# Expert stage of a hybrid encoder layer on one Trainium2 core: the loop over slots written out, and each expert number read once

## What is computed

```python
def _hier_moe(x, w_rg, b_rg, w_re, b_re, w1, w3, w2):
    ...
    y = jnp.zeros(t.shape, jnp.float32)
    for e in range(N_EXPERTS):
        he = jax.nn.silu(t @ w1[e]) * (t @ w3[e])
        y = y + gates[:, e:e + 1] * (he @ w2[e]).astype(jnp.float32)
    return y.reshape(B, S, D).astype(x.dtype)
```

## Time and profile before

| what | value |
| --- | --- |
| median of 3 runs | 1200.32 us (1195.77 to 1204.63) |
| the profiled execution | 1196.12 us, of which the span from first to last instruction is 1194.2 us |
| PE busy over the span | 1065.5 us (89%) |
| DVE, ACT, POOL busy | 697.2, 525.4, 344.9 us |
| mean granted clock of PE | 0.962 |
| DMA, mean over the span | 203 GB/s |
| DMA on SP's queue (q1), on POOL's (q0) | 117.42 MB, 122.17 MB |

### The profile page before, as it was taken

One profiled execution on the slowest core, in us unless ns is written; L12 is line 12 of the kernel. 1 busy time (PEld: TensorE's weight loads), 2 busy tenths in 40 slices (PEclk: granted clock), 3 DMA queues, 4 the chain that ended last, 5 costly groups with the idle time before them and its releaser, 6 DMA issues.

```text
span 1194.2 us, 18236 instructions
## 1 busy us (share of the span) xinstructions
PE 1065.5 (89%) x5777; PEld 860.0 (72%) x5777; DVE 697.2 (58%) x1326; ACT 525.4 (44%) x1025; POOL 344.9 (29%) x368
## 2 busy tenths in 40 slices
PE   5999999998987899999999999975999999999940
PEld 4889889984555777777778777863777777777830
DVE  4330610118666667576575655448777777787867
ACT  4432421213532333323333333313787878788823
POOL 3100510000541111111110100201656565666655
PEclk9999999999989999899999999996999999999985
DMA  7340141122579586465555444834988687877667
GB/s 273 118 164 1 45 127 64 45 78 68 195 272 364 199 322 244 174 229 207 205 198 198 156 170 151 295 143 160 302 313 325 243 282 248 284 253 255 246 240 278
DMA packets 105764, 242.83 MB, mean 203 GB/s; under 512 B 15248, under 2 KB 63840, under 8 KB 95456
## 3 DMA queue, kind: packets, MB, share of 16 engines
q1 hardware_dynamic: 81312, 117.42, 28.8%
q0 software_dynamic: 23328, 122.17, 28.7%
q10 hardware_dynamic: 1056, 2.36, 0.6%
HBM read 243.31 MB, written 48.94 MB: 245 GB/s over the span
## 4 chain that ended last, share of the span: by engine, by line
PE 58%; DMA 12%; DVE 9%; issue 8%; ACT 5%; SPq 5%; POOL 2%; POOLq 0%; DVEq 0%; ACTq 0%
DMA below<-in_w 8%; PE ps L1076 5%; PE ps L2189 4%; PE ps L2191 4%; PE ps L2190 4%; PE ps L929 4%; PE ps L947 3%; SPq L1426 3%; PE ps L1117 3%; PE ps L1025 3%; PE ps L1118 3%; PE ps L2184 3%; PE ps L2183 3%; PE ps L2185 3%; PE ps L1121 3%
## 5 line engine op out<-in xcount | busy, mean ns | idle before, releaser
L1842 DVE TENSOR_TENSOR low<-below,high 128x1024 fp32r<-128x1024 f32 x128 | 156.6, 1260 | 35.3 <-ACT high L1539 31.8
L1638 PE MATMUL ps<-high 128*128 128x512 f32 x384 | 156.1, 407 | 10.8 <-DVE low L1852 7.2
L1514 POOL TENSOR_TENSOR low<-below,high 128x1024 fp32r<-128x1024 f32 x62 | 129.0, 2081 | 94.0 <-ACT high L1559 93.1
L1639 PE MATMUL ps<-low,high 128*128 128x512 f32 x384 | 150.7, 392 | 0.0
L1640 PE MATMUL ps<-high,low 128*128 128x512 f32 x384 | 150.6, 392 | 0.0
L1539 ACT ACTIVATE high<-below 128x1024 fp32r<-128x1024 f32 x128 | 130.3, 1070 | 38.6 <-DMA below<-in_w 37.9
L653 ACT ACTIVATE arena<-ps 128x512 f32<-128x512 f32 (+8 forms) x100 | 50.1, 511 | 172.0 <-PE ps L929 171.6
L929 PE MATMUL ps<-arena 128*128 128x128 f32 (+4 forms) x613 | 94.3, 277 | 7.5 <-ACT arena L653 2.2
L797 POOL DMA_DIRECT2D high<-wo_dram x34 | 18.7, 549 | 281.6 <-PE ps L1121 270.8
L1638 PEld LDWEIGHTS ps<-high 128*128 128x128 f32 x384 | 72.5, 189 | 28.1 <-issue 12.8
L947 PE MATMUL ps<-arena 128*128 128x64 f32 (+2 forms) x624 | 83.4, 269 | 6.9 <-DVE arena L702 2.9
(11 more groups left out here) (251 smaller groups left out, 2215.8 us busy)
## 6 DMA issues: line engine op xcount, KB each, us to landing
below<-in_w SPq DMA_DIRECT2D x256, 256.0 KB
high<-wo_dram POOLq DMA_DIRECT2D x36, 1024.0 KB, 5.9
low<-wo_dram POOLq DMA_DIRECT2D x36, 1024.0 KB, 8.6
below<-in_w POOLq DMA_DIRECT2D x64, 512.0 KB
y_dram<-arena SPq DMA_DIRECT2D x32, 512.0 KB
arena<-in_x_prompt SPq DMA_DIRECT2D x15, 512.0 KB
below<-in_w_in SPq DMA_DIRECT2D x14, 512.0 KB, 7.7
out<-arena SPq DMA_DIRECT2D x9, 512.0 KB, 2.7
```

Of the source, the lines that this page charges most:

```text
L1514: pool.tensor_tensor(w2_lo[s % UN][:, c], w2_in[:, c], w2_hi[s % UN][:, c].bitcast(F32), ALU.subtract).then_inc(s_w2lo, 1)
L1638: pe.matmul(out, x_hi, w_hi, start=start, stop=False)
L1639: pe.matmul(out, x_hi, w_lo, start=False, stop=False)
L1842: dve.tensor_tensor(chunk(w13_lo[j], c), chunk(w13_in, c), chunk(w13_hi[j], c).bitcast(F32), ALU.subtract).then_inc(s_w13lo, 1)
```

## The change

`expert_turns` is replaced by `expert_slots`, which writes all 32 slots out for ACT, PE and DVE, with every slot number a constant. SP's body becomes a plain loop over 32 slots that is written out in the same way. `expert` takes the number of the slot before as an argument (a register that was loaded a slot earlier) and loads only one number. On SP the number of slot s+1 is read after the loads of slot s are issued and ahead of the wait for the output rows of s-3; the second wait for `s_etab`, which had been there in every slot, goes. On POOL it is read after the gather and ahead of the two subtractions. What each engine computes, and in which order, is otherwise as it was.

```diff
-    def expert_turns(eng, body):
-
-        turns = SLOT_TILES // UN - 1
-        assert SLOT_TILES % UN == 0
-        for it in range(2):
-            for j in range(UN):
-                body(it, j, it == 0, False)
-        with eng.Fori(2, turns - 1) as it:
-            for j in range(UN):
-                body(it, j, False, False)
-        for it in (turns - 1, turns):
-            for j in range(UN):
-                body(it, j, False, it == turns and j == UN - 1)
+    def expert_slots(body):
+
+        for s in range(SLOT_TILES):
+            body(s // UN, s % UN, s < UN, s == SLOT_TILES - 1)
...
-    def expert(eng, s):
-
-        e = eng.value_load(expert_of[0:1, bass.ds(s, 1)], min_val=0, max_val=NE - 1)
-        if is_zero(s):
-            return e, None
-        return e, e != eng.value_load(expert_of[0:1, bass.ds(s - 1, 1)], min_val=0, max_val=NE - 1)
+    def expert(eng, s, e_before):
+
+        e = eng.value_load(expert_of[0:1, s:s + 1], min_val=0, max_val=NE - 1)
+        return e, None if e_before is None else e != e_before
 
     def moe_loads(sp):
...
         sp.wait_ge(s_etab, 1)
-
-        def body(it, j, first, last):
-            s = it * UN + j
-            e, new = expert(sp, s)
+        e, new = expert(sp, 0, None)
+        for s in range(SLOT_TILES):
+            j = s % UN
             rows13 = [w[0, bass.ds(e, 1)].rearrange("e (c p) f -> p (e c) f", p=P) for w in (w1, w3)]
             for c in range(WC):
 
-                if not is_zero(s):
-                    split = sp.to_reg(WC * (s - 1) + c + 1)
-                    if c == 0:
-
-                        sp.wait_ge(s_etab, 1)
-
-                    sp.wait_ge(s_w13lo, split)
+                if s:
+                    sp.wait_ge(s_w13lo, WC * (s - 1) + c + 1)
                 for k in range(2):
                     sp.dma_start(w13_in[:, 2 * c:2 * c + 2, k * FF:(k + 1) * FF], rows13[k][:, 2 * c:2 * c + 2, :],
                                  cond=new).then_inc(s_w13in[c], 16)
-            if not isinstance(s, int) or s >= 3:
+            if s + 1 < SLOT_TILES:
+                e, new = expert(sp, s + 1, e)
+            if s >= 3:
                 store_y(s - 3)
...
-        def load_second(s):
-            e, new = expert(pool, s)
+        def load_second(s, e, new):
...
             if s + 1 < SLOT_TILES:
+                e, new = expert(pool, s + 1, e)
                 for c in range(2):
                     pool.wait_ge(s_w2hi, 2 * s + c + 1)
                     pool.tensor_tensor(w2_lo[s % UN][:, c], w2_in[:, c], w2_hi[s % UN][:, c].bitcast(F32),
                                        ALU.subtract).then_inc(s_w2lo, 1)
-                load_second(s + 1)
+                load_second(s + 1, e, new)
```

More of the change, by code:

```diff
@@ L1400, in chunk @@
         return w[:, 2 * c:2 * c + 2, :]
-    def expert(eng, s):
-        e = eng.value_load(expert_of[0:1, bass.ds(s, 1)], min_val=0, max_val=NE - 1)
-        if is_zero(s):
-            return e, None
-        return e, e != eng.value_load(expert_of[0:1, bass.ds(s - 1, 1)], min_val=0, max_val=NE - 1)
-    def moe_loads(sp):
-        sp.wait_ge(s_etab, 1)
-        def body(it, j, first, last):
-            s = it * UN + j
-            e, new = expert(sp, s)
-            rows13 = [w[0, bass.ds(e, 1)].rearrange("e (c p) f -> p (e c) f", p=P) for w in (w1, w3)]
-            for c in range(WC):
-                if not is_zero(s):
-                    split = sp.to_reg(WC * (s - 1) + c + 1)
-                    if c == 0:
-                        sp.wait_ge(s_etab, 1)
-                    sp.wait_ge(s_w13lo, split)
-                for k in range(2):
-                    sp.dma_start(w13_in[:, 2 * c:2 * c + 2, k * FF:(k + 1) * FF], rows13[k][:, 2 * c:2 * c + 2, :],
-                                 cond=new).then_inc(s_w13in[c], 16)
-            if not isinstance(s, int) or s >= 3:
[L1429 to L1436, removed]
+    def expert(eng, s, e_before):
+        e = eng.value_load(expert_of[0:1, s:s + 1], min_val=0, max_val=NE - 1)
+        return e, None if e_before is None else e != e_before
+    def moe_loads(sp):
         def store_y(s):
@@ L1444, in load_res @@
             sp.dma_start(res[t][0:R, :], h1_dram[t * P:t * P + R, :]).then_inc(s_res, 16)
-        expert_turns(sp, body)
+        sp.wait_ge(s_etab, 1)
+        e, new = expert(sp, 0, None)
+        for s in range(SLOT_TILES):
+            j = s % UN
+            rows13 = [w[0, bass.ds(e, 1)].rearrange("e (c p) f -> p (e c) f", p=P) for w in (w1, w3)]
+            for c in range(WC):
+                if s:
+                    sp.wait_ge(s_w13lo, WC * (s - 1) + c + 1)
+                for k in range(2):
+                    sp.dma_start(w13_in[:, 2 * c:2 * c + 2, k * FF:(k + 1) * FF], rows13[k][:, 2 * c:2 * c + 2, :],
+                                 cond=new).then_inc(s_w13in[c], 16)
+            if s + 1 < SLOT_TILES:
+                e, new = expert(sp, s + 1, e)
+            if s >= 3:
+                store_y(s - 3)
+                sp.dma_start(y_dram[(s - 3) * P:(s - 2) * P, :], y_row[:, (j + 1) % UN, :]).then_inc(
+                    s_yst[(j + 1) % UN], 16)
+            if s == EARLY:
+                sp.wait_ge(s_h1st, 16 * NT)
+                sp.wait_ge(s_slots, 2)
+                for t in range(NT):
+                    load_res(t)
         for s in range(SLOT_TILES - 3, SLOT_TILES):
@@ L1504, in moe_pool @@
         gather(0)
-        load_second(0)
+        e, new = expert(pool, 0, None)
+        load_second(0, e, new)
         gather(1)
@@ L1589, in body @@
                            ACT.Copy).then_inc(s_mga, 1)
-        expert_turns(act, body)
+        expert_slots(body)
         free_last(act)
@@ L1697, in body @@
             ins.then_inc(s_mgt, 1)
-        expert_turns(pe, body)
+        expert_slots(body)
         down(SLOT_TILES - 1, (SLOT_TILES - 1) % UN)
@@ L1902, in body @@
                               ALU.subtract).then_inc(s_mgv, 1)
-        expert_turns(dve, body)
+        expert_slots(body)
         first_adds(range(2))
```

## The result

The changed kernel takes 1207.98 us (median of 15 runs, 1203.93 to 1212.27) against 1201.40 us (15 runs, 1194.47 to 1209.55) for the kernel before on the same chip: a ratio of 1.0059, 95% interval 1.0043 to 1.0075. The forecast was 1196 with a range of 1187 to 1204, so the sign was wrong and the time lies outside the range; the loss stays under 1%. The two profiled executions, 1210.88 and 1196.12 us, lie further apart than the medians. They show where the time goes; how much it is, the medians say.

What follows compares the result with a forecast made beforehand. PE was taken as the bound, its waits in the expert stage costing 15.1 us. Only SP's earlier load counted: 1196.12 − 4.2 = 1191.9 us, or 1196 on the footing of the runs' median; range 1187 to 1204.

Steps and rivals of the forecast that it cites:

- What bounds the kernel: Expert stage: PE busy 276.34 of 286.50 us, held up by the last w1/w3 chunk's landing; all waits cost 15.1 us.
- SP comes earlier: SP's first load issued 0.4 us after DVE's first subtraction, not 0.87; the last chunk issued 0.7 us earlier.
- the price of the earlier load: Last chunk's earlier issue on SP: 0.35 us gained in each of 12 stalls, 4.2 us; bounds 0 and 8.4 us.
- Rival three: Earlier w1/w3 loads push back w2, ACT's split and the Silu; 1.0 us free, beyond it 6 us slower, 1206; chance 0.06.
- Instruction fetch: Fetching of written-out code, judged on PE's queue q8, two blocks from 1110 to 1150 us: value 0.
- Rival four: Fetches stall the written-out engines behind full DMA queues: 12 more PE blocks at 1 us, 12 us slower, 1212; chance 0.06.
- the sum: Profiled 1196.12 minus 4.2 us gives 1191.9; on the footing of the runs' median, 4.2 us higher, 1196.1.
- POOL: POOL's number load moves ahead of its two subtractions and one of two goes: value 0, bound 3.6 us of gain.
- ACT's and DVE's branches: Loop ends gone with PE, ACT and DVE written out: value 0, bound 2.5 us of gain from PE's branch.
- SP's read ahead of the output-row wait: One number load of 0.27 to 0.87 us before that wait, covered by its average 1.6 us: costs nothing.

Runs made afterwards that it cites:

- e2: Kernel before with SP alone as after the change (written out, one number load, read ahead of the output-row wait); ratio 1.0046.
- e6: e2 with three useless number reads on SP ahead of its first load of a slot; ratio 0.9986 to the kernel before.
- e18: e13 with e2's SP code (written out and early); ratio 1.0028 to the kernel before.
- e13: Kernel before with two useless number reads on POOL ahead of each gather from slot 2 on; ratio 0.9998.
- e8: Kernel before with PE alone written out; ratio 1.0029.
- e12: Kernel before with ACT and DVE written out and PE in its loop; ratio 0.9986.
- e3: Kernel before with POOL's new code alone, its number read ahead of the two subtractions; ratio 1.0001.
- e16: Kernel before with POOL, from slot 3 on, issuing an even slot's gather ahead of its two subtractions, not behind the w2 loads; 0.9964, 1195.31 us against 1199.82.
- e17: e16 with e2's SP code (written out and early); ratio 0.9981 to the kernel before.
- e10: e9 with e2's SP code (written out and early); ratio 0.9893 to the kernel before.
- e9: Kernel before without the gathers of slots 2 to 31, all slots computing on the first two slots' rows; ratio 0.9886.
- e11: Kernel before with POOL issuing each half of w2 behind its own subtraction and reading the expert numbers ahead of both; ratio 1.0146.
- e14: Kernel before with PE in a loop of four slots a turn instead of two; ratio 1.0022.

## Why the prediction was wrong, point by point

**What bounds the kernel: right.** PE was held up in slots with a load by the landing of the last chunk, and the time lost appears there and nowhere else; slots without a load kept their 9.4 us.

**SP comes earlier: right, and of no value.** 0.4 us behind DVE was forecast, 0.34 measured. For the last chunk, though, the forecast had the issue 0.7 us earlier. Counted from w2's issue it came 0.2 us earlier (6.5 for 6.7 us; 6.3 in e2), as SP took 5.0 us from its first issue to its eighth instead of 4.7. The step that failed is the price of the earlier load: "an earlier load mostly takes turns with bytes that must move before the last chunk lands anyway. Lower bound: nothing, as the engines are full." Its value was +0.35 us in each stalled slot; the changed kernel shows a loss of 1.1 us there, e2, with SP's part alone, one of 0.6. The gain was bounded by the order of issue, and the order of issue wasn't the bound: in e6 the last chunk lands as early with SP 1.2 us later than before. The loss was excluded with no reason that a row bears out. Engines that are full say that an early request gains nothing; they don't say that it takes nothing from a stream ahead of it. Nor did the reading allow for 16 engines that finish unevenly. The windows of the earlier trace rows show a mean over them, and ACT waits for the last landing.

**Rival three: the right stream, the wrong path.** It named w2 as the stream that would be pushed back, and it is: e18 against e13 has its second half 0.6 us later, e2 against the kernel before 0.9. The rival let up to 1.0 us of that pass as free, and by that nothing would have been lost. Its path led by the Silu that stands behind w2's split. What happened instead is that the last chunk of w1/w3 landed later, which e2 and e18 have in common. Why a load 0.5 us earlier leaves its landings more spread out stays open. By the rule of the Trainium skill that the prediction quotes ("DMA: Bandwidth & Descriptors", "Queues, rings and completion order"), w2 would lose half of the overlap, by the prediction's estimate 0.25 us; the trace of the change shows 0.6 us (second half landed at 6.7 for 6.1), and the measurement decides.

**Instruction fetch: "Value 0", wrong by some 0.3%.** PE written out alone costs 1.0029 [1.0008, 1.0051]. Rival four probably had the cause, and the wrong mechanism: it expected PE to stall for its own instructions, "PE idle by 'issue' with packets on q8 beside it". The packets are there, 9 from 880 to 1110 us where it counted 12 and the kernel before has none, but PE waits for the product, as it does when a chunk is late. The forecast looked for the fetch at the engine that asks for it, not at the DMA engine that carries it. By the rule of the Trainium skill on a taken branch ("Runtime: NRT & Kernel Launch", "Instruction fetch mechanics") the written-out loop should have gained if the branch's target had to be fetched. The trace before has no packet of q8 from 874 to 1117 us, so PE's branch fetched nothing, and e8 and e12 show no gain on any of the three engines.

**What the sum left out: the clock.** In the changed kernel a late chunk is sometimes paid for twice. From 1100 to 1105 us:

```profile
1100.00:1105.00 5.00, 3.69 (x11) 2.77 (x12) 4.05 (x7) 5.00 (x10) 4.68 (x3) 0.71 0.25 105
```

PE has stood still for 1.37 and 0.47 us, and the granted clock then falls to 0.5, 1.2 GHz, for 3.4 us; that slot takes 13.2 us. The stretch before has no such place. The forecast priced a microsecond of waiting at a microsecond.

**Right at nothing:** POOL (e3, 1.0001), ACT's and DVE's branches (e12, 0.9986), and SP's read ahead of the output-row wait, which stayed covered (SP still waits there 38.5 us in 30 waits, for 45.6 in 28).

## What to carry to other kernels

When several streams feed one stage, ask of a load that comes earlier not only what it gains but whose bytes it runs against, and put a negative lower bound on it until a run has delayed the same load on purpose: one useless read on the issuing engine told here that the lead was worth nothing. Look for the gap in which the DMA engines stand idle (0.29 busy from 969 to 975.2 us before, in one slot) and move the transfer that nobody waits for into it, as e16 did; that was the only edit here that leaves no step out and made the kernel faster. And count what code brings with it: blocks of written-out instructions use the DMA engines that carry the data.

## What the runs showed of the hardware that was not expected

- An issue 0.5 us earlier on one queue made the last landing of the last chunk 0.4 to 0.7 us later, with equal bytes and the first landing of that chunk unchanged at 11.5 us (e2 and e18 against the kernel before and e13). With the gather moved away or left out it was 0.1 to 0.2 us (e17 against e16, e10 against e9).
- A block of PE's instructions is 16 KB and took 0.9 to 1.4 us of one DMA engine (eleven of them in the changed kernel).
- PE idle for 1.70 us, then 0.48 (e8), was followed by 3.4 us at a granted clock of 0.5, with 0.63 in place of 0.39 us for a 128x512 matmul. Not every such gap was: in the changed kernel PE resumed at 1038.38 after 1.93 us, stood still 0.48 again, and kept its clock.
- DVE's 128x1024 subtraction took 2.2 to 3.1 us instead of 1.22 in 21 of 23 cases in which a 128x1024 subtraction of POOL ran beside it for 1 us or more, and 1.22 beside POOL's DMA issues (e11).
- Four slots of PE's code in a loop, twice that of before, brought no block of instructions from 910 to 1110 us (e14).
